# Two more places for expert panels: 23 in place of 21, from the scratch for dynamic DMAs

## The chip, the cores and the metric

The kernel runs on one core of one Trainium2 chip. The metric is the time of one execution on the device in microseconds, taken as the median of several runs. The core has TensorE for matrix products, VectorE, ScalarE and GpSimd for the rest, SyncE (SP), which here issues nearly all loads, and 16 DMA engines. Its on-chip memory, SBUF, has 128 partitions.

## What is computed

Two layers over 256 tokens of width 1024, in float32, batch 1. The first layer is a hybrid of a sparse latent attention (16 heads, top 64 keys) and a gated linear recurrence; the second has two attentions (MLA and MoBA, 8 heads each) and a mixture of 32 experts, of which each token uses two. Cut to what matters:

```python
def reference(x, ...):
    x = first_block(x, ...)     # x + (g_a * y_attn + g_r * y_rnn) @ w_out, then rms_norm
    return second_block(x, ...)

def second_block(x, ...):
    ...
    x = x + mixed @ w_out[l]
    x = x + hierarchical_moe(rmsnorm(x, ffn_norm[l]), ..., w_exp_gate[l], w_exp_up[l], w_exp_down[l])
    return rmsnorm(x, final_norm)

def expert_block(args):         # once for each expert, with its own three weights
    xb, e = args
    return (jax.nn.silu(xb @ w_g[e]) * (xb @ w_u[e])) @ w_d[e]
```

Each expert has a gate and an up weight of 1024 x 256 and a down weight of 256 x 1024. The weights of all 32 experts are read, 96 MB (3 MB for each expert), and the weights of the dense stages are another 70 MB.

## The kernel before

The dense weights come in 70 panels of 1 MB (`w_dense[p]`, 128 x 2048), each of two units of 128 x 1024. They go through the first four slots of `ring` (`DRING = 4`). ScalarE copies a unit into a rounded form (line 1165), GpSimd takes the difference between unit and rounded form (line 1579), and TensorE multiplies three times with these parts (`mm3`, line 509). Each unit that TensorE finishes raises `unit_done`. Dense panel p is loaded when the units of the panel in its slot are done: `dense_laps(a, b)` (line 404) does so in a loop, four slots a lap.

The expert weights come in 96 panels of 1 MB (`w_expert[q]`, `PANELS = 96`), six for each pair of experts: four with the gate and up weights (two halves of the depth for each expert), two with the down weights. They go through `wide_ring` (line 244), a list of `NSLOT` = 21 places of 8 KB per partition. Panel q uses place q mod `NSLOT`. The list holds tensors that the dense stages need earlier and that have become free: `wu`, parts of `small` and `big`, `scr`, `hT`, `attn`, the constants, the slots of `ring`, and `xT`. `expert(q)` (line 411) loads a panel, `expert_half(q, k)` (line 414) half of one, and `expert_panel(eng, q)` (line 360) is the wait of its reader. `in_halves` names the panels of the first filling that are loaded in two halves.

SP issues everything in one written order: the loads of the start (lines 389 to 400), then laps of dense panels with an expert panel between them where a place becomes free. `expert(0)` stands behind the keys of the first layer, `expert(1)` and `expert(2)` in the second layer, the other 18 towards the end of the dense stages. From line 470 on come the reloads, q from 21 to 95 in steps of two: each waits until `panel_used` says that panels q-21 and q-20 have been used. TensorE raises `panel_used` in `gate_up_half` (line 982), `sw_transposes` (line 972), `down` (line 1033) and `add_experts` (line 1073). Behind the last panel comes the last gain (line 488), 512 KB, which VectorE reads in the output stage (`layer_out`, line 2088).

In the expert layer TensorE goes through 16 pairs. A pair has two halves of gate and up products (line 993), two transposes, the down products (line 1041) and the sum into the output's banks (`add_experts`, line 1076); the next group's tokens are gathered between (line 968). The last two pairs also have idle products (`idle_products`, line 999), whose results nobody reads. The last pair's down products are those of `last_down` (line 1047).

Semaphores of the small weights: `s_in["wuk"]` and `s_in["wuv"]` for two loads into `wu`, `s_in["wkr"]` and `s_in["wrt"]` for two more.

The kernel is built with the default scratch for dynamic DMAs, 16 KB per partition of SBUF, which lies ahead of all tensors.

Of the kernel before, what the change touches and what calls it, by code (L numbers as in the profile page):

```python
# [30 lines left out]
P = 128  # L31
T = 256
NT = T // P
D = 1024
DC = D // P
# [24 lines left out]
PANELS = 3 * NE  # L60
CAUSAL = P + T

UNIT = 1024
RING = 6
DRING = 4
# [14 lines left out]
FILL0, UNIT0, UNITS_AT, RELEASE = {}, {}, [], []  # L80
# [40 lines left out]
def build(nc, x_t, vecs, consts, w_rg, w_uk, w_uv, w_kr, w_router, w_dense, w_expert, final_row, out):  # L121
    ctx = ExitStack()
    with ctx:
        def sb(name, shape, dt=F32):
            return ctx.enter_context(nc.sbuf_tensor(name, shape, dt))

        def sem(name):
            return ctx.enter_context(nc.semaphore(name))
# [3 lines left out]
        def sb2(name, shape):  # L132

            offset = -(-nc.sbuf_base // 32) * 32
            t = sb(name, shape)
            rounded[name] = nc.alloc_sbuf_tensor_at(f"{name}_r", shape, F32R, offset=offset)
            return t
# [18 lines left out]
        stat = sb("stat", [P, 2, 3, 2])  # L156
        th = sb("th", [P, 2, 2 * T])
        small = sb2("small", [P, 5 * 1024])

        def at(region, off, *dims):  # L160
            n = 1
# [74 lines left out]
        def xe_block(g, half, couple):  # L236
# [4 lines left out]
        x1_sq = at(small, 2 * K, DC, T)  # L241
        ye = at(small, 3 * K, 2, 512)
        sel = wkr.rearrange("p c n -> p (c n)").rearrange("p (a b c) -> p a b c", a=2, b=NT)
        wide_ring = [wu[:], small[:, 0:2 * K], big[:, 16 * K + 512:18 * K + 512], scr.rearrange("p c t -> p (c t)"), hT.rearrange("p c t -> p (c t)"),
                     attn[:, 0:2 * UNIT], cst[:, CST["center"]:CST["center"] + 2 * K],
                     big[:, 4 * K:6 * K], big[:, 6 * K:8 * K], big[:, 0:2 * K],
                     big[:, 14 * K:16 * K], big[:, 12 * K:14 * K], ring[:, 2, :], ring[:, 3, :], ring[:, 0, :],
                     ring[:, 4, :], ring[:, 1, :], ring[:, 5, :], big[:, 10 * K:12 * K], big[:, 2 * K:4 * K],
                     xT.rearrange("p c t -> p (c t)")]
        NSLOT = len(wide_ring)  # L250
        last_gain = wide_ring[12][:, 0:D]
        in_halves = {14, 15, 16, 17, 20}
        last_couple = 6 * (PAIRS - 1)
        rt = at(small, 4 * K, 1024)

# [3 lines left out]
        def C(name, n, i=0):  # L259
# [6 lines left out]
                                          for n in ("D0", "D1", "L0", "L1", "TB", "QB", "OB", "UB")]  # L266
# [13 lines left out]
        SPLITS = ("x0", "x", "u", "o", "m1", "x1", "att2", "wkr", "cq", "ck", "ob", "oa", "m2")  # L280
        hi_of = {n: sem(f"{n}_rounded") for n in SPLITS}
        lo_of = {n: sem(f"{n}_rest_ready") for n in SPLITS}
        s_in = {n: sem(f"in_{n}") for n in ("x0", "x1", "vec", "cst", "wrg", "wuk", "wuv", "wkr", "wrt",
                                            "first_unit", "last_gain")}
        unit_done, panel_used = sem("unit_done"), sem("expert_panel_used")
        rel = {"act": sem("bank_released_by_act"), "dve": sem("bank_released_by_dve")}
# [97 lines left out]
        @block.sync  # L384
        def _(sp_):
            def panel(slot, src):
                return sp_.dma_start(ring[:, slot, :], src).then_inc(arrived[slot], 16)

            sp_.dma_start(vec[:], vecs).then_inc(s_in["vec"], 16)
            sp_.dma_start(dense_unit(0), w_dense[0][:, 0:UNIT]).then_inc(s_in["first_unit"], 16)  # L390
            sp_.dma_start(xT[:, 4:8, :], x_half(1)).then_inc(s_in["x1"], 16)
            sp_.dma_start(dense_unit(1), w_dense[0][:, UNIT:2 * UNIT]).then_inc(arrived[0], 16)
            sp_.dma_start(cst[:, 0:NCST], consts).then_inc(s_in["cst"], 16)
            for p in range(1, DRING):
                panel(p, w_dense[p])
            sp_.dma_start(wrg, w_rg.rearrange("p (a c t) -> p a c t", a=2, c=8)).then_inc(s_in["wrg"], 16)
            sp_.dma_start(wuk, w_uk.rearrange("p (c t) -> p c t", c=8)).then_inc(s_in["wuk"], 16)
            sp_.dma_start(wuv, w_uv.rearrange("p (c t) -> p c t", c=16)).then_inc(s_in["wuv"], 16)
            sp_.dma_start(wkr[:], w_kr.rearrange("p (c t) -> p c t", c=DC)).then_inc(s_in["wkr"], 16)
            sp_.dma_start(wrt[:], w_router.rearrange("p (c t) -> p c t", c=DC)).then_inc(s_in["wrt"], 16)  # L400

            laps = DENSE_PANELS // DRING - 1

            def dense_laps(a, b):
                with sp_.Fori(a, b) as lap:
                    for slot in range(DRING):
                        sp_.wait_ge(unit_done, lap * (2 * DRING) + (2 * slot + 2 - 2 * DRING))
                        sp_.dma_start(ring[:, slot, :], w_dense[bass.ds(lap * DRING + slot, 1)].rearrange(
                            "a p n -> p (a n)")).then_inc(arrived[slot], 16)

            def expert(q):
                sp_.dma_start(wide_ring[q % NSLOT], w_expert[q]).then_inc(earrived[q % NSLOT], 16)

            def expert_half(q, k, arrival=None):
                part = np.s_[:, k * UNIT:(k + 1) * UNIT]
                sp_.dma_start(wide_ring[q % NSLOT][part], w_expert[q][part]).then_inc(arrival or earrived[q % NSLOT], 16)

            lap_keys = UNIT0["aproj"] // (2 * DRING) + 1
            lap_latents = UNIT0["qb"] // (2 * DRING) + 2
            lap_rotated = UNIT0["gates"] // (2 * DRING) + 1  # L420
            dense_laps(1, lap_keys)
            sp_.wait_ge(kk_mm, H1 // 2)
            expert(0)
            dense_laps(lap_keys, lap_latents)
            sp_.wait_ge(unit_done, UNIT0["qb"])
            expert(1)
            dense_laps(lap_latents, lap_rotated)
            sp_.wait_ge(maxed, H1 + 1)
            expert(2)
            dense_laps(lap_rotated, laps)  # L430

            def dense(p):
                sp_.wait_ge(unit_done, 2 * (p - DRING) + 2)
                panel(p % DRING, w_dense[p])

            left = list(range(laps * DRING, DENSE_PANELS))
            dense(left.pop(0))
            dense(left.pop(0))
            sp_.wait_ge(unit_done, UNIT0["omoba"])
            expert(3)  # L440
            expert(4)
            dense(left.pop(0))
            dense(left.pop(0))
            sp_.wait_ge(o_mm, H1 + 2 * H2)
            expert(5)
            expert(6)
            expert(7)
            dense(left.pop(0))
            expert(8)
            dense(left.pop(0))  # L450

            sp_.wait_ge(unit_done, UNIT0["out2"])
            expert(9)
            expert(10)
            sp_.wait_ge(mixed, 8)
            expert(11)
            for q, units in ((12, 134), (13, 136)):
                sp_.wait_ge(unit_done, units)
                expert(q)
            for q in (14, 16):  # L460
                for k in range(2):
                    sp_.wait_ge(unit_done, 137 + q - 14 + k)
                    expert_half(q, k)
                    expert_half(q + 1, k)
            expert(18)
            expert(19)
            for k in range(2):
                sp_.wait_ge(x2_in, 2 * k + 2)
                expert_half(20, k)
            for q in range(NSLOT, PANELS, 2):  # L470
                freed = 2 * (q - NSLOT)
                if q in in_halves:
                    for k in range(2):
                        sp_.wait_ge(panel_used, freed + 2 * k + 2)
                        expert_half(q, k)
                        expert_half(q + 1, k)
                else:
                    sp_.wait_ge(panel_used, freed + 4)
                    for n in range(q, min(q + 2, PANELS)):
                        if n in second_half:  # L480
                            expert_half(n, 0)
                            if n != last_couple + 2:
                                if n == last_couple + 3:
                                    expert_half(n - 1, 1, second_half[n - 1])
                                expert_half(n, 1, second_half[n])
                        else:
                            expert(n)
            sp_.wait_ge(panel_used, 2 * (PANELS - 2 * NSLOT + 22))
            sp_.dma_start(last_gain, final_row).then_inc(s_in["last_gain"], 16)

            for tt in range(NT):
                sp_.wait_ge(out_scaled, tt + 1)
                sp_.dma_start(out[:, (2 * tt + 1) * 512:(2 * tt + 2) * 512], y_out[:, tt, 512:1024]).then_inc(stored, 16)
            sp_.wait_ge(stored, 16 * 2 * NT)
# [3 lines left out]
        def _(pe):  # L498
# [178 lines left out]
                   wu[:, UNIT + (n % 2) * 512:UNIT + (n % 2 + 1) * 512], start=True, stop=True).then_inc(v1_mm, 1)  # L677

            pe.wait_ge(s_in["wrg"], 16)
            pe.wait_ge(s_in["wuv"], 16)  # L680
            for c in range(8):
                chunk("q", c, h2, between=(lambda i: rg_gates(3 * c - 16 + i)) if c >= 6 else None)
                if 2 <= c < 6:
# [51 lines left out]
                else:  # L735
                    chunk("rproj", rtodo.pop(0), (u_hi, u))

            pe.wait_ge(s_in["wuk"], 16)
            kept(pe, "q", 3)
            pe.wait_ge(v1_ready, 4)  # L740
            pe.wait_ge(widx_ready, 1)
# [166 lines left out]
            for i in range(4):  # L908
                half_chunk("omla", i, (oa_hi, oA))
            pe.wait_ge(padz, 1)  # L910
            pe.wait_ge(s_in["wrt"], 16)

            def route(i):

# [670 lines left out]
        def _(dve):  # L1585
# [284 lines left out]
            fold(cq_sq, 1, SQ0[N_CQ] + 2)  # L1870
            dve.wait_ge(sq, SQ0[N_CQ] + 3)
            v.tensor_tensor(cq_sq[:, 0:2, :], cq_sq[:, 0:2, :], cq_sq[:, 4:6, :], ALU.add).then_inc(cq_folded, 1)
            dve.wait_ge(s_in["wkr"], 16)
            split("wkr", wkr, wkr_hi, 0, DC)
            dve.wait_ge(s_in["wrt"], 16)
            v.tensor_tensor(wrt[:], wrt[:], V("ffn_norm_2", 0, 8).unsqueeze(2).to_broadcast([P, DC, NG + NE]),
                            ALU.mult).then_inc(padz, 1)

# [384 lines left out]
```

## Time and profile before

| | |
|---|---|
| median of 3 runs | 707.6 us (707.43 to 707.69) |
| span of the profiled execution | 705.3 us |
| TensorE (PE) busy | 660.1 us, 94% |
| GpSimd (POOL), VectorE (DVE), ScalarE (ACT) busy | 379.2, 335.9, 326.9 us |
| data moved by DMA | 181.71 MB, mean 258 GB/s |
| chain that ended last | PE 80%, DMA 14% |

The profile is of one execution; the page gives its span, and no time around it, so the median is set beside the span. Lines with SPq are instructions of SP's queue, which issues loads; the second number is how long the issue took, not the transfer. PEclk is TensorE's granted clock, 1.00 for 2.4 GHz and 0.50 for 1.2 GHz. The DMA share is the mean busy share of the 16 DMA engines in a window; rounding can take it to 1.01 and above. A number in square brackets at the end of a line is idle time ahead of the instruction and what ended it.

### The profile page before, as it was taken

The numbers are of one execution on the slowest core, as the hardware profiler recorded it, in microseconds if no ns is written. First come the engines' busy times: TensorE is split into PE (matmuls) and PEld (weight loads), VectorE is DVE, ScalarE is ACT, GpSimd is POOL, SyncE is SP. The second block draws the span as 40 slices with busy tenths as digits, with TensorE's granted clock in tenths as the row PEclk, the third lists the DMA queues.
The fourth block names the chain that finished last, engine by engine and source line by source line (L and its number), as shares of the span: only waits on it lengthen the run. The fifth ranks groups of instructions, "written<-read, shape, count | busy, mean of one in ns | idle before, by whom it ended". The sixth has DMA issues, their size and how long they took to land.

```text
span 705.3 us, 13837 instructions
## 1 busy us (share of the span) xinstructions
PE 660.1 (94%) x5608; PEld 550.3 (78%) x5608; DVE 335.9 (48%) x684; ACT 326.9 (46%) x603; POOL 379.2 (54%) x284
## 2 busy tenths in 40 slices
PE   5999999999999999999999999999999998687894
PEld 4899899999999999998899999999654544343442
DVE  5869723787871247895754554443422121121102
ACT  6566777866554456664358655442311111010104
POOL 3988557798887989998697555882000000000000
PEclk9999999999999999999999999999999999999998
DMA  8845334435346555464457334799899999999994
GB/s 341 322 168 180 119 121 132 168 122 172 125 158 210 184 189 188 158 245 166 141 167 285 126 120 157 309 425 388 346 423 419 422 422 419 423 423 420 422 419 162
DMA packets 27281, 181.71 MB, mean 258 GB/s; under 512 B 3024, under 2 KB 3280, under 8 KB 6864
## 3 DMA queue, kind: packets, MB, share of 16 engines
q1 hardware_dynamic: 26784, 179.74, 66.4%
q8 instruction: 47, 0.77, 0.5%
q10 hardware_dynamic: 432, 1.05, 0.4%
q14 instruction: 18, 0.15, 0.1%
HBM read 179.73 MB, written 1.05 MB: 256 GB/s over the span
## 4 chain that ended last, share of the span: by engine, by line
PE 80%; DMA 14%; ACT 2%; DVE 2%; issue 0%; POOL 0%; SPq 0%; ACTq 0%; DVEq 0%
PE D L512 49%; PE L L993 5%; DMA cst<-w_expert_dram 4%; DMA big<-w_expert_dram 4%; DMA ring<-w_expert_dram 4%; PE L L968 3%; PE L L696 2%; PE QB L1041 2%; PE D L560 2%; DMA ring<-w_dense_dram 2%; PE TB L705 2%; PE D L1076 1%; PE L L1002 1%; PE TB L1076 1%; PE L L668 1%; PE D L564 1%
## 5 line engine op out<-in xcount | busy, mean ns | idle before, releaser
L1579 POOL TENSOR_TENSOR ring_r<-ring,ring_r 128x512 fp32r<-128x512 f32 (+1 forms) x280 | 379.0, 1388 | 100.2 <-ACT ring_r L1165 99.7
L512 PE MATMUL D<-scr_r,ring_r 128*128 128x256 f32 x1104 | 214.0, 289 | 0.0
L1165 ACT ACTIVATE ring_r<-ring 128x1024 fp32r<-128x1024 f32 (+2 forms) x140 | 145.1, 1042 | 93.4 <-PE D L512 80.4
L512 PEld LDWEIGHTS D<-scr_r,ring_r 128*128 128x128 f32 x1104 | 175.6, 191 | 2.4 <-issue 1.6
L512 PE MATMUL D<-hT_r,ring_r 128*128 128x256 f32 x552 | 156.1, 283 | 0.0
L512 PE MATMUL D<-big_r,ring_r 128*128 128x256 f32 x1086 | 134.1, 284 | 1.7 <-POOL ring_r L1579 1.7
L512 PEld LDWEIGHTS D<-big_r,ring_r 128*128 128x128 f32 x1086 | 131.3, 192 | 3.4 <-POOL ring_r L1579 2.4
L512 PEld LDWEIGHTS D<-hT_r,ring_r 128*128 128x128 f32 x552 | 105.7, 192 | 1.1 <-issue 0.7
L1596 DVE SCALAR_TENSOR_TENSOR th<-th,L 64x256 f32<-64x256 f32 x32 | 13.4, 418 | 128.2 <-ACT th L1501 127.7
L1501 ACT ACTIVATE th<-L 64x256 f32<-64x256 f32 x16 | 6.0, 377 | 84.5 <-PE L L993 84.5
L993 PE MATMUL L<-big,small 128*32 128x256 f32 x384 | 34.5, 395 | 5.5 <-DMA ring<-w_expert_dram 3.0
L968 PEld LDWEIGHTS L<-wkr,big 128*128 128x128 f32 x240 | 27.9, 191 | 10.6 <-issue 9.9
L1321 ACT ACTIVATE attn<-TB 128x384 f32<-128x384 f32 x32 | 15.7, 491 | 39.0 <-PE TB L705 39.0
L968 PE MATMUL L<-wkr,big 128*128 128x128 f32 x240 | 30.6, 281 | 0.6 <-DVE wkr L2016 0.6
L1596 DVE SCALAR_TENSOR_TENSOR big<-big,D 128x512 f32<-128x512 f32 x16 | 11.0, 685 | 38.0 <-PE D L512 38.0
L1504 ACT ACTIVATE root<-OB 128x128 f32<-128x128 f32 x16 | 4.4, 278 | 52.7 <-PE OB L1030 52.7
L993 PEld LDWEIGHTS L<-big,small 128*32 128x32 f32 x384 | 17.3, 113 | 14.3 <-issue 7.7
L1313 ACT ACTIVATE L<-L,stat 128x128 f32<-128x128 f32 x64 | 25.1, 393 | 3.3 <-DVE stat L1726 3.2
L993 PE MATMUL L<-ring,small 128*32 128x256 f32 x256 | 21.2, 403 | 5.7 <-DMA ring<-w_expert_dram 2.9
L2053 DVE TENSOR_TENSOR small<-L,vec 128x256 f32<-128x256 f32 x30 | 11.3, 419 | 27.9 <-PE L L968 27.9
L1735 DVE TENSOR_SCALAR attn<-L,stat 128x128 f32<-128x128 f32 x64 | 23.8, 413 | 1.1
L1507 ACT ACTIVATE small<-QB 128x512 f32<-128x512 f32 x15 | 9.0, 597 | 30.6 <-PE QB L1041 30.6
(393 smaller groups left out, 1014.7 us busy)
## 6 DMA issues: line engine op xcount, KB each, us to landing
ring<-w_dense_dram SPq DMA_DIRECT2D x69, 1024.0 KB, 5.0
big<-w_expert_dram SPq DMA_DIRECT2D x35, 1024.0 KB, 23.8
ring<-w_expert_dram SPq DMA_DIRECT2D x20, 1024.0 KB, 26.2
wu<-w_expert_dram SPq DMA_DIRECT2D x5, 1024.0 KB, 24.4
small<-w_expert_dram SPq DMA_DIRECT2D x5, 1024.0 KB, 21.7
scr<-w_expert_dram SPq DMA_DIRECT2D x5, 1024.0 KB, 24.7
hT<-w_expert_dram SPq DMA_DIRECT2D x5, 1024.0 KB, 26.4
attn<-w_expert_dram SPq DMA_DIRECT2D x5, 1024.0 KB, 26.6
```

The source lines that it names most:

```text
L512: last = mm(out_, r32(w[i][ws]), r32(x[j][xs_]), start=start and m == 0, stop=stop and m == 2)
L560: mm(bank[:, u * T:(u + 1) * T], r32(w[h][:, k * P:(k + 1) * P]), r32(src[0][:, k, :]), start=(u + k + h == 0), stop=False, skip_group_che ...
L696: last = mm(LB[j][:, c0:c0 + n], q_of(j, tt), k_of(j, n), start=True, stop=True)
L705: last = nc.tensor.transpose(TB[:, b * P:(b + 1) * P], E[:, a % 2, b * P:(b + 1) * P], ident)
L968: last = mm(into[:, c * P:(c + 1) * P], htok[:, tt, (c0 + c) * P:(c0 + c + 1) * P], sel[:, g % 2, tt, :], start=(tt == 0), stop=(tt == NT ...
L993: last = mm(G[at_:at_ + WIN, 0:FF], x(4 * h + k, e), w[e][:, k, m, :], start=(h + k == 0), stop=(h * 4 + k == DC - 1))
L1165: A_(r32(hi_unit(j)[w]), dense_unit(j)[w], ACT.Copy).then_inc(hi_ready, 1)
L1313: last = A_(LB[a % 2][:, c0:c0 + n], LB[a % 2][:, c0:c0 + n], ACT.Exp, bias=stat[:, a % 2, 0, tt:tt + 1], accum_out=stat[:, a % 2, 1, tt:t ...
L1321: A_(PT[:, a % 2, :], TB[:, 0:CAUSAL], ACT.Copy).then_inc(pt_ready, 1)
L1579: last = g.tensor_tensor(r32(w), w, r32(h).bitcast(F32), ALU.subtract)
L1596: return v.scalar_tensor_tensor(out=out_, in0=in0, scalar=scalar, in1=in1, op0=op0, op1=op1)
L1735: last = v.tensor_scalar(E[:, a % 2, c0:c0 + n], LB[a % 2][:, c0:c0 + n], stat[:, a % 2, 2, tt:tt + 1], None, ALU.mult)
```

## The change

A tensor `spare` of two places is added, and the scratch for dynamic DMAs is set to 1024 bytes, which frees 15 KB of the 16 KB that it needs. The two places go to the front of `wide_ring`, so `NSLOT` is 23 and each old place has a number two higher. Panels 0 and 1 are loaded into them in the first layer, behind the first lap of dense panels (`UNIT0["gattn"]` is 22, so `lap_spare` is 2); each old place of the first filling gets the panel with a number two higher at the old point. The reloads run from 23 to 95. The last gain goes to the place of panel 73. Two pairs of small loads share a semaphore each, and their readers wait for both.

```diff
+        spare = sb("spare", [P, 2, 2 * UNIT])
...
-        wide_ring = [wu[:], small[:, 0:2 * K], big[:, 16 * K + 512:18 * K + 512], ...
+        wide_ring = [spare[:, 0, :], spare[:, 1, :], wu[:], small[:, 0:2 * K], big[:, 16 * K + 512:18 * K + 512], ...
...
-        last_gain = wide_ring[12][:, 0:D]
-        in_halves = {14, 15, 16, 17, 20}
+        last_gain = wide_ring[(PANELS - NSLOT) % NSLOT][:, 0:D]
+        in_halves = {16, 17, 18, 19, 22}
...
-            sp_.dma_start(wuk, w_uk.rearrange("p (c t) -> p c t", c=8)).then_inc(s_in["wuk"], 16)
-            sp_.dma_start(wuv, w_uv.rearrange("p (c t) -> p c t", c=16)).then_inc(s_in["wuv"], 16)
-            sp_.dma_start(wkr[:], w_kr.rearrange("p (c t) -> p c t", c=DC)).then_inc(s_in["wkr"], 16)
-            sp_.dma_start(wrt[:], w_router.rearrange("p (c t) -> p c t", c=DC)).then_inc(s_in["wrt"], 16)
+            sp_.dma_start(wuk, w_uk.rearrange("p (c t) -> p c t", c=8)).then_inc(s_in["wuk_wuv"], 16)
+            sp_.dma_start(wuv, w_uv.rearrange("p (c t) -> p c t", c=16)).then_inc(s_in["wuk_wuv"], 16)
+            sp_.dma_start(wkr[:], w_kr.rearrange("p (c t) -> p c t", c=DC)).then_inc(s_in["wkr_wrt"], 16)
+            sp_.dma_start(wrt[:], w_router.rearrange("p (c t) -> p c t", c=DC)).then_inc(s_in["wkr_wrt"], 16)
...
+            lap_spare = UNIT0["gattn"] // (2 * DRING)
...
-            dense_laps(1, lap_keys)
+            dense_laps(1, lap_spare)
+            expert(0)
+            expert(1)
+            dense_laps(lap_spare, lap_keys)
             sp_.wait_ge(kk_mm, H1 // 2)
-            expert(0)
+            expert(2)
...
-            sp_.wait_ge(panel_used, 2 * (PANELS - 2 * NSLOT + 22))
+            sp_.wait_ge(panel_used, 2 * (PANELS - NSLOT + 1))
             sp_.dma_start(last_gain, final_row).then_inc(s_in["last_gain"], 16)
...
-            pe.wait_ge(s_in["wuv"], 16)
+            pe.wait_ge(s_in["wuk_wuv"], 32)
...
-            dve.wait_ge(s_in["wkr"], 16)
+            dve.wait_ge(s_in["wkr_wrt"], 32)
...
-    nc = bacc.Bacc("TRN2", target_bir_lowering=False, num_devices=1)
+    nc = bacc.Bacc("TRN2", target_bir_lowering=False, num_devices=1, dynamic_dma_scratch_size=1024)
```

## Rows read from the trace of the kernel before

**Rows 1.** Windows of all engines by stage, the first line naming the columns.
```profile
core 0: us, PE busy (x) PEld busy (x) DVE busy (x) ACT busy (x) POOL busy (x), PEclk, DMA share, GB/s
500.00:580.00 80.00, 77.08 (x848) 42.10 (x840) 20.17 (x67) 11.69 (x31) 0.00 (x0) 1.00 0.98 405
580.00:660.00 80.00, 60.24 (x610) 31.02 (x614) 10.88 (x33) 8.51 (x22) 0.00 (x0) 0.94 1.01 422
660.00:692.00 32.00, 30.90 (x254) 13.80 (x250) 3.67 (x10) 5.20 (x12) 0.00 (x0) 0.98 1.00 411
```

**Rows 2.** Timeline of TensorE, 590 to 660 us: instructions behind a wait for a panel.
```profile
start us, us, engine line op out<-in xcount [idle before <-releaser]
597.48 1.93 PE L993 MATMUL L<-ring,small 128*32 128x256 f32 x32 [2.94 <-DMA ring<-w_expert_dram]
...
607.41 1.93 PE L993 MATMUL L<-big,small 128*32 128x256 f32 x32 [1.22 <-DMA big<-w_expert_dram]
...
613.44 0.61 PE L993 MATMUL L<-xT,small 128*32 128x256 f32 x1 [4.10 <-DMA wu<-w_expert_dram]
...
628.32 0.38 PE L993 MATMUL L<-attn,small 128*32 128x256 f32 x1 [2.68 <-DMA cst<-w_expert_dram]
...
643.20 0.38 PE L993 MATMUL L<-big,small 128*32 128x256 f32 x1 [3.04 <-DMA ring<-w_expert_dram]
...
658.15 0.61 PE L993 MATMUL L<-ring,small 128*32 128x256 f32 x1 [2.73 <-DMA big<-w_expert_dram]
```

**Rows 3.** Chain that ended last, in order of time: start, us, what.
```profile
658.15 3.40 PE L L993 x32
...
692.95 0.86 PE L L1056 x16
```

**Rows 4.** Timeline of SP's queue (issues of loads); below, a landing from the DMA view.
```profile
501.81 0.33 SPq L412 DMA_DIRECT2D wu<-w_expert_dram  x1
...
594.62 2.13 SPq L412 DMA_DIRECT2D hT<-w_expert_dram  x1
...
675.06 2.13 SPq L489 DMA_DIRECT2D ring<-final_row_dram  x1
...
ring<-final_row_dram SPq DMA_DIRECT2D x1, 512.0 KB, 19.1
```

**Rows 5.** Windows of all engines where the reloads begin.
```profile
500.00:502.00 2.00, 2.00 (x34) 1.10 (x27) 0.95 (x6) 0.00 (x0) 0.00 (x0) 1.00 0.14 51
502.00:504.00 2.00, 2.00 (x32) 1.45 (x34) 1.61 (x8) 0.00 (x0) 0.00 (x0) 1.00 0.53 131
```

**Rows 6.** The page: DMA queue with share; issues with median us to landing.
```profile
q1 hardware_dynamic: 26784, 179.74, 66.4%
...
ring<-w_expert_dram SPq DMA_DIRECT2D x20, 1024.0 KB, 26.2
```

**Rows 7.** SP's and ScalarE's timelines, landing of the loads of line 408, a window.
```profile
39.31 0.33 SPq L408 DMA_DIRECT2D ring<-w_dense_dram  x1
48.48 0.33 SPq L408 DMA_DIRECT2D ring<-w_dense_dram  x1
57.04 1.06 ACT L1165 ACTIVATE ring_r<-ring 128x1024 fp32r<-128x1024 f32 x1 [0.51 <-PE D L512]
DMA to landing us min/median/max: 4.7/4.8/4.9
40.00:50.00 10.00, 10.00 (x88) 9.16 (x87) 7.15 (x22) 8.10 (x16) 6.89 (x7) 1.00 0.38 116
```

**Rows 8.** A landing from the DMA view, and TensorE's timeline: first value product.
```profile
wrt<-w_router_dram SPq DMA_DIRECT2D x1, 144.0 KB, 18.8
...
68.30 1.02 PE L676 MATMUL OB<-wu,small 128*128 128x512 f32 x2
```

**Rows 9.** Windows of all engines behind two of the waits.
```profile
614.00:616.00 2.00, 2.00 (x25) 0.98 (x21) 0.00 (x0) 0.00 (x0) 0.00 (x0) 0.50 1.03 430
658.00:660.00 2.00, 1.85 (x20) 1.07 (x24) 0.00 (x0) 0.00 (x0) 0.00 (x0) 0.50 1.02 430
```

More of the change, by code:

```diff
@@ L243, in build @@
         sel = wkr.rearrange("p c n -> p (c n)").rearrange("p (a b c) -> p a b c", a=2, b=NT)
-        wide_ring = [wu[:], small[:, 0:2 * K], big[:, 16 * K + 512:18 * K + 512], scr.rearrange("p c t -> p (c t)"), hT.rearrange("p c t -> p (c t)"),
+        wide_ring = [spare[:, 0, :], spare[:, 1, :], wu[:], small[:, 0:2 * K], big[:, 16 * K + 512:18 * K + 512], scr.rearrange("p c t -> p (c t)"), hT.rearrange("p c t -> p (c t)"),
                      attn[:, 0:2 * UNIT], cst[:, CST["center"]:CST["center"] + 2 * K],
@@ L282, in build @@
         lo_of = {n: sem(f"{n}_rest_ready") for n in SPLITS}
-        s_in = {n: sem(f"in_{n}") for n in ("x0", "x1", "vec", "cst", "wrg", "wuk", "wuv", "wkr", "wrt",
+        s_in = {n: sem(f"in_{n}") for n in ("x0", "x1", "vec", "cst", "wrg", "wuk_wuv", "wkr_wrt",
                                             "first_unit", "last_gain")}
@@ L420, in _ @@
             lap_rotated = UNIT0["gates"] // (2 * DRING) + 1
-            dense_laps(1, lap_keys)
+            dense_laps(1, lap_spare)
+            expert(0)
+            expert(1)
+            dense_laps(lap_spare, lap_keys)
             sp_.wait_ge(kk_mm, H1 // 2)
-            expert(0)
+            expert(2)
             dense_laps(lap_keys, lap_latents)
             sp_.wait_ge(unit_done, UNIT0["qb"])
-            expert(1)
+            expert(3)
             dense_laps(lap_latents, lap_rotated)
             sp_.wait_ge(maxed, H1 + 1)
-            expert(2)
+            expert(4)
             dense_laps(lap_rotated, laps)
@@ L439, in _ @@
             sp_.wait_ge(unit_done, UNIT0["omoba"])
-            expert(3)
-            expert(4)
+            expert(5)
+            expert(6)
             dense(left.pop(0))
@@ L444, in _ @@
             sp_.wait_ge(o_mm, H1 + 2 * H2)
-            expert(5)
-            expert(6)
             expert(7)
+            expert(8)
+            expert(9)
             dense(left.pop(0))
-            expert(8)
+            expert(10)
             dense(left.pop(0))
             sp_.wait_ge(unit_done, UNIT0["out2"])
-            expert(9)
-            expert(10)
+            expert(11)
+            expert(12)
             sp_.wait_ge(mixed, 8)
-            expert(11)
-            for q, units in ((12, 134), (13, 136)):
+            expert(13)
+            for q, units in ((14, 134), (15, 136)):
                 sp_.wait_ge(unit_done, units)
                 expert(q)
-            for q in (14, 16):
+            for q in (16, 18):
                 for k in range(2):
-                    sp_.wait_ge(unit_done, 137 + q - 14 + k)
+                    sp_.wait_ge(unit_done, 137 + q - 16 + k)
                     expert_half(q, k)
                     expert_half(q + 1, k)
-            expert(18)
-            expert(19)
+            expert(20)
+            expert(21)
             for k in range(2):
                 sp_.wait_ge(x2_in, 2 * k + 2)
-                expert_half(20, k)
+                expert_half(22, k)
             for q in range(NSLOT, PANELS, 2):
@@ L736, in fill @@
                     chunk("rproj", rtodo.pop(0), (u_hi, u))
-            pe.wait_ge(s_in["wuk"], 16)
+            pe.wait_ge(s_in["wuk_wuv"], 32)
             kept(pe, "q", 3)
@@ L910, in _ @@
             pe.wait_ge(padz, 1)
-            pe.wait_ge(s_in["wrt"], 16)
+            pe.wait_ge(s_in["wkr_wrt"], 32)
             def route(i):
@@ L1872, in _ @@
             v.tensor_tensor(cq_sq[:, 0:2, :], cq_sq[:, 0:2, :], cq_sq[:, 4:6, :], ALU.add).then_inc(cq_folded, 1)
-            dve.wait_ge(s_in["wkr"], 16)
+            dve.wait_ge(s_in["wkr_wrt"], 32)
             split("wkr", wkr, wkr_hi, 0, DC)
-            dve.wait_ge(s_in["wrt"], 16)
+            dve.wait_ge(s_in["wkr_wrt"], 32)
             v.tensor_tensor(wrt[:], wrt[:], V("ffn_norm_2", 0, 8).unsqueeze(2).to_broadcast([P, DC, NG + NE]),
```

## The prediction

> **What bounds the kernel now.** I read the stages first, then TensorE's waits inside the last stage, then the queue that feeds it.
>
> The windows by stage [rows 1] split the last 200 us in three. From 500 to 580 TensorE is busy 77.08 of 80 us and the DMA engines 98% of the time: both run nearly full. From 580 to 660 the DMA engines have a share of 1.01 and move 422 GB/s, and TensorE is busy only 60.24 of 80 us: here the stream of expert panels sets the pace. From 660 to 692 both are full again. This is the expert layer: 96 panels of 1 MB pass through 21 places, and TensorE eats six of them (one pair of experts) in less time than the DMA engines bring six.
>
> TensorE's own timeline [rows 2] has seven waits for a panel between 597 and 658 us, of 2.94, 1.22, 4.10, 2.68, 1.20, 3.04 and 2.73 us (the fifth, at 638.23, isn't shown), 17.91 us in all, and none after 658.15. Four of them end at 613.44, 628.32, 643.20 and 658.15: 14.88, 14.88 and 14.95 us apart. Between two of them lies the work of one pair of experts, so six panels arrive in 14.9 us, 2.48 us each. The bandwidth says the same: 1,048,576 bytes at 422 GB/s are 2.485 us, and I take that.
>
> The chain that ended last [rows 3] tells what follows. From 658.15 TensorE works without a wait for data to the last down products at 692.95; then come the sums, squares, scale and store, to the span's end at 705.3. The chain doesn't show that the last panel is due at the same moment. The last gain, issued behind it at 675.06, lands after 19.1 us, at 694.2 [rows 4]. It is half a megabyte, 1.24 us at this rate, so the second half of panel 95 lands at about 692.9, and TensorE wants it in the second half of the products that begin at 692.95. So the last stage has two ends that meet within half a microsecond, TensorE's work behind 658.15 and the last byte of the stream, and both hang on the stream.
>
> **The change part by part.**
>
> *Two panels fewer in the stream.* Before, panels 0 to 20 are loaded ahead and 75 go into places that must be freed first; after, 23 and 73. What counts is when these reloads start and how fast they run. They start when TensorE has used panels 0 and 1: the first is issued at 501.81 [rows 4], and that doesn't depend on how many places there are. The loads ahead stay where they are, with numbers two higher: place k of before is place k+2 of after and is filled at the same point of the program. In the windows [rows 5] the DMA engines have nothing left at 500 (share 0.14), take up the reloads until 504 (0.53), and are full from there on. SP runs ahead of them: the issue at 501.81 took 0.33 us, that at 594.62 took 2.13 us, as long as the queue needs to make room [rows 4], and loads into the ring land 26.2 us after their issue [rows 6], some ten panels later. So the stream is limited by its rate, not by free places, and panel q arrives when q-2 arrived before: 2 x 2.485 = 4.97 us earlier. The bounds are 4.96 us (a third of 14.88) and 5.10 us (at the 411 GB/s of the last window of [rows 1]).
>
> Does TensorE follow? I replay its timeline [rows 2] with arrivals 4.97 us earlier. First wait: ready at 597.48 - 2.94 = 594.54, panels at 592.5, no wait. Second: ready at 607.41 - 1.22 - 2.94 = 603.25, panels at 602.4, none. Third: ready at 613.44 - 4.10 - 1.22 - 2.94 = 605.18, panels at 613.44 - 4.97 = 608.47: it waits 3.29 us, and from here on every time is that of before less 4.97. The last wait ends at 653.18, the last panel lands at 687.9, and the work behind them is unchanged. Gain: 4.97 us; 17.91 - 4.97 = 12.9 us of waits stay. What is late next is the same stream at the same place.
>
> *The two loads in the first layer.* They are issued behind the load of 39.31, the fourth of the first lap, so within a microsecond of it; the next load in the ring is issued at 48.48, when ten units are done, and SP has nothing to do between [rows 7]. A load alone lands after 4.8 us [rows 7]: the load of 39.31 at 44.1, and the two new ones, each 2.485 us later, at 46.6 and 49.1. The data of the load of 48.48 starts 4.8 - 2.5 = 2.3 us after its issue, when they are through. The window from 40 to 50 has a DMA share of 0.38 [rows 7], so 6.2 us free where 4.97 are wanted. If they did collide, the panel of 48.48 (landing at 53.3) is first read by ScalarE at 57.04 [rows 7]: 3.7 us of slack, and the rounding itself runs ahead of TensorE. Cost 0, the bound above is 4.97 - 3.7 = 1.3 us.
>
> *The scratch of 1 KB.* It moves every tensor 15 KB down and gives the room for the two places. All weights travel on queue q1, of kind hardware dynamic: 179.74 of 181.71 MB [rows 6]; no line of the kernel issues a DMA from GpSimd. Cost 0 by these rows, with a rival below. The Trainium skill, "DMA: Bandwidth & Descriptors", section "SWDGE vs HWDGE vs iDMA", says that this carveout holds the descriptor rings that GpSimd writes, and that loads from SP and ScalarE don't use it; by that page its size costs nothing, and no run here shows that yet.
>
> *The merged semaphores.* Each wait now ends with the later of two loads, all issued before 9 us; the last of the four lands 18.8 us after its issue, so by 28 us, and the first reader of any of them that I find is the value product at 68.30 [rows 8]. Cost 0.
>
> *The last gain* goes to the fifth place of the new list and waits for panel 73 rather than 75, but SP reaches that wait only behind the issue of panel 95, which waits for as much. It stays behind the stream and comes 4.97 us earlier. Cost 0. One loop on SP becomes two, in an idle stretch of 8 us. Cost 0.
>
> *Sum.* The profiled span 705.3 - 4.97 = 700.3 us. The median of the runs shown, 707.6, lies 2.3 us above the span; with the same 2.3 around it, 702.6 us. The Trainium skill, "DMA: Bandwidth & Descriptors", section "Bandwidth", puts the HBM side at about 358 GB/s per core when both cores of a domain stream; by that figure two panels would be worth an estimated 5.9 us and the time would be 701.7. The trace moves 422 GB/s with one core at work, and the sum goes by that.
>
> **The rivals.**
>
> *The clock falls once more behind the last wait.* TensorE's granted clock is 0.50, the lower of its two levels, in 614 to 616 and in 658 to 660, both right behind a wait for a panel [rows 9]. The 32 matmuls behind the wait of 607.41 took 1.93 us [rows 2], those behind 658.15 took 3.40 [rows 3]: 1.47 us lost. After the change the waits lie differently (two are gone, one is 3.29 in place of 4.10), so a drop can come at another moment. One is in the path already; one more between the last wait and the end costs 1.5 us, two cost 2.9: 704.1 to 705.5 us. Against it: from 660 to 692 TensorE is busy 30.90 of 32 us at a clock of 0.98 [rows 1]. If the present drop goes away, TensorE is 1.5 us earlier but the last panel isn't, and the gain grows by 0.3 at most, to 702.3. The Trainium skill, "TensorE: Matmul & The Clock Gate", section "HAM oscillation — how this bites in real kernels", says that waits for DMA between short bursts of products bring the slow clock back every time; the trace agrees in part, since after the wait of 607.41 the products ran at full speed.
>
> *The extra loads only push the others.* If they held up the dense ring and it never caught up, the 4.97 us would be spent there: 707.6 us. For it: the first layer is TensorE's and its ring is only four panels deep. Against it: 0.38 of the DMA engines used where the loads go.
>
> *Only part arrives*, because the reloads start later or with gaps: with half of the gain, 705.1 us. For it: the start of the reloads is set by a release, not by the rate [rows 4, 5]. Against it: nothing moves that release.
>
> *Slower: the small scratch limits the loads in flight.* If the 1 KB also held the descriptors of these loads, the ten or so in flight would become few. A load alone takes 4.8 us [rows 7] against 2.485 in the stream, so down to two in flight nothing is lost and below two it decides: with one, 73 x 4.8 = 350 us in place of 75 x 2.485 = 186, 164 us more, about 872 us. Against it: the kind of the queue [rows 6].
>
> *The change doesn't do what it says*: the two places are new memory, so nothing can be in the way of the early loads; if they were issued late instead, that is the case of the part gain.
>
> **How the numbers follow.** Forecast 702.6 (its own range 702.0 to 703.3): 0.77. A further drop of the clock (704.1 to 705.5): 0.10. Part of the gain (705.1): 0.05. No gain (707.6): 0.04. Slower, by the scratch or something that no row shows: 0.04. The range is 702.0 to 704.6: below, the bound of 5.10, the 0.3 of a missing drop and the spread of 0.26 us of the runs; above, one further drop. A measurement of this kernel can tell about 0.2%, 1.4 us, from no change. Faster by more: 0.91; within: 0.05; slower by more: 0.04.
>
> **What would show it.** In the profile after: the first reload issued at 501.8 as before; DMA share 1.01 and 422 GB/s until about 685 in place of 690; TensorE's first wait for a panel near 608, five waits in all of about 13 us, the last ending near 653.2; two expert loads issued behind 39.3 and the ring's next still at 48.5. The prediction is wrong if the stage until 500 is longer, if the products behind 653 run at the low clock for longer than before, or if loads of the expert stream land after 5 us where 26 were usual.

## The result

The changed kernel takes 701.98 us (median of 4 runs, 701.08 to 702.66) beside 707.51 us for the kernel before (706.80 to 707.69): ratio 0.9922, with a 95% interval of 0.9900 to 0.9944. That is 5.5 us less, between 4.0 and 7.1. The direction and the mechanism were forecast; the size, 4.9 to 5.0 us, was too small by half a microsecond, and the median lies 0.02 us below my range. The profiled execution took 701.36 us with a span of 699.6 us, so some 1.8 us lie around the span, not 2.3 as I had set from a span and a median of different executions. My sum takes the 2.3 off and adds it again, so this changes nothing in it.

The windows of the profile after, with the columns of [rows 1]; the second and third stage are taken 5 us earlier than there:

```profile
500.00:580.00 80.00, 77.07 (x840) 41.73 (x832) 19.40 (x61) 11.68 (x31) 0.00 (x0) 1.00 1.00 411
575.00:655.00 80.00, 62.78 (x646) 33.55 (x642) 12.75 (x39) 8.78 (x23) 0.00 (x0) 0.96 1.01 422
655.00:687.00 32.00, 30.90 (x258) 13.88 (x254) 3.67 (x10) 5.19 (x12) 0.00 (x0) 0.99 0.98 401
```

The stream still moves 422 GB/s, and TensorE still waits for it: 62.78 of 80 us busy, against 60.24 before. TensorE's timeline, as in [rows 2], has six waits now, of 3.95, 2.64, 1.20, 3.02, 1.17 and 3.04 us, 15.0 us in all:

```profile
607.55 3.29 PE L998 MATMUL L<-ring,small 128*32 128x256 f32 x32 [3.95 <-DMA ring<-w_expert_dram]
622.41 0.38 PE L998 MATMUL L<-xT,small 128*32 128x256 f32 x1 [2.64 <-DMA spare<-w_expert_dram]
...
652.13 3.48 PE L998 MATMUL L<-big,small 128*32 128x256 f32 x32 [3.04 <-DMA big<-w_expert_dram]
```

The first two waits of before are gone. The last ends at 652.13 in place of 658.15: 6.02 us earlier, where I had said 4.97. SP's queue, as in [rows 4] and [rows 7], says where the rest comes from:

```profile
39.70 0.80 SPq L413 DMA_DIRECT2D spare<-w_expert_dram  x2
48.46 166.43 SPq L409 DMA_DIRECT2D ring<-w_dense_dram  x24
...
500.51 0.80 SPq L413 DMA_DIRECT2D spare<-w_expert_dram  x2
503.69 0.33 SPq L413 DMA_DIRECT2D wu<-w_expert_dram  x1
```

The two early loads go out at 39.7, and the next dense one still at 48.46. But the first reload goes out at 500.51, not 501.81. It waits for TensorE, and TensorE was earlier because of its clock. Windows of all engines in the routing stage ahead of the expert layer, first of the kernel before, then of after:

```profile
490.00:492.00 2.00, 2.00 (x13) 2.00 (x13) 1.08 (x9) 0.26 (x1) 0.00 (x0) 0.62 0.92 301
492.00:494.00 2.00, 2.00 (x12) 2.00 (x12) 1.76 (x12) 0.82 (x2) 0.00 (x0) 0.52 1.03 399
```

```profile
490.00:492.00 2.00, 2.00 (x20) 2.00 (x20) 1.12 (x9) 0.79 (x2) 0.00 (x0) 1.00 0.99 348
492.00:494.00 2.00, 2.00 (x19) 1.86 (x17) 1.76 (x12) 1.53 (x3) 0.00 (x0) 1.00 1.01 397
```

The third number from the right is the granted clock: 0.62 and 0.52 before, 1.00 and 1.00 after. The first number in brackets counts TensorE's products: 25 in four microseconds before, 39 after. What I had to find out was whether the change did that, or chance.

Some single executions are delayed by 2 to 6 us (twelve of 64 of the kernel before, none of 16 of the changed kernel, one to three in each of five of its variants); the medians include them, and the profiles compared here are free of such a delay unless I say so.

### The profile page after: what moved, and what is told of

Same layout as the page of the kernel before. It is cut to its first block, busy times and chain, and to the rows that moved or that the text cites. A ratio compares the mean times of both kernels' runs of the same rounds, so it can differ in the third digit from the quotient of the medians.

```text
span 699.6 us, 13827 instructions
## 1 busy us (share of the span) xinstructions
PE 657.5 (94%) x5608; PEld 549.2 (79%) x5608; DVE 334.3 (48%) x684; ACT 326.8 (47%) x603; POOL 379.1 (54%) x284
## 4 chain that ended last, share of the span: by engine, by line
PE 83%; DMA 10%; DVE 2%; ACT 2%; issue 1%; SPq 0%; POOL 0%; ACTq 0%; DVEq 0%
PE D L517 49%; PE L L998 6%; DMA spare<-w_expert_dram 4%; DMA big<-w_expert_dram 4%; PE L L973 3%; PE QB L1046 3%; PE L L701 2%; PE D L565 2%; PE D L1081 2%; DMA ring<-w_dense_dram 2%; PE TB L710 2%; PE TB L1081 1%; PE L L1007 1%; PE L L673 1%; PE D L569 1%; PE D L548 1%
## 5 line engine op out<-in xcount | busy, mean ns | idle before, releaser
L998 PE MATMUL L<-big,small 128*32 128x256 f32 x368 | 31.9, 400 | 4.2 <-DMA big<-w_expert_dram 4.2
L998 PE MATMUL L<-ring,small 128*32 128x256 f32 x256 | 18.3, 406 | 4.0 <-DMA ring<-w_expert_dram 4.0
```

The lines of the kernel that those rows point to most:

```text
L998: last = mm(G[at_:at_ + WIN, 0:FF], x(4 * h + k, e), w[e][:, k, m, :], start=(h + k == 0), stop=(h * 4 + k == DC - 1))
```

## The experiments

The theories. *Stream*: the time is the bytes that the reload stream has to move, behind the moment at which it starts; two panels less are 4.97 us. *Chance*: the rest is TensorE's clock, which falls ahead of the reloads in some executions of either kernel. Against them: the change prevents the fall; the moved addresses or the small scratch bring a part; the number of places counts for something other than bytes; TensorE's work behind the last wait is the bound, not the stream.

**The changed kernel again, twice.** No edit.

> The changed kernel once more, with many runs beside the kernel before. Two theories for the 0.7 us beyond the 4.97 us of two panels. Clock by chance: TensorE's clock falls to 0.50 between 490 and 494 us in some executions and not in others, whichever kernel it is, and each fall costs 1.3 us; then single runs of either kernel lie in two groups 1.3 us apart (changed: about 701.2 and 702.6, before: about 706.3 and 707.6), each group with its own mean clock, and groups of the same clock differ by 5.0 us. The change removes the fall: the kernel before is always near 707.5 and the changed one always near 701.2, a gain of 6.3 us in fast pairs.

> The changed kernel once more, to stand beside the two below and to give more single runs for the two levels. If the fall of the clock before 494 us comes by chance in either kernel: again some runs near 701.3 and some near 702.6, and of before some near 706.2 and some near 707.4, like groups 4.8 to 5.0 us apart; the share of each group may be any.

Ratios 0.9923 (0.9908 to 0.9938) and 0.9923 (0.9907 to 0.9939), medians 702.09 and 702.14. With the four runs of the result there are 16 single runs of the changed kernel: seven from 700.99 to 701.85 (median 701.36), nine from 702.11 to 703.29 (702.60). Of 64 runs of the kernel before, 21 lie from 705.38 to 706.80 (median 706.18), 31 from 706.95 to 708.27 (707.46), twelve from 709.22 to 712.54. So both kernels have a lower and an upper group 1.2 to 1.3 us apart. They aren't sharply divided, and I drew the lines at 706.85 and at 702.1 by eye. Like compared with like, the gain is 706.18 - 701.36 = 4.8 and 707.46 - 702.60 = 4.9 us. Without a line between the groups it is the same: the means, the twelve slowest left out, are 707.02 and 702.07, 4.95 us apart. That speaks for chance and against a fall that the change prevents. The printed clock of a run is only a loose sign of its group.

The profile of the first of the two has the fall, in the same place as before, and its last wait is 1.40 us later than in the profile after. Its windows, SP's queue and TensorE's timeline:

```profile
490.00:492.00 2.00, 2.00 (x17) 2.00 (x17) 1.01 (x8) 0.68 (x2) 0.00 (x0) 0.84 1.00 291
492.00:494.00 2.00, 2.00 (x11) 2.00 (x11) 1.76 (x14) 0.96 (x2) 0.00 (x0) 0.50 1.03 399
```

```profile
501.89 0.80 SPq L413 DMA_DIRECT2D spare<-w_expert_dram  x2
```

```profile
653.53 1.93 PE L998 MATMUL L<-big,small 128*32 128x256 f32 x32 [2.89 <-DMA big<-w_expert_dram]
```

Against the kernel before with the same fall (first reload at 501.81, last wait ending at 658.15) that is 4.62 us, with nearly the same start of the reloads. One of the two groups isn't always this fall, though. The second profile (702.57 us) has no fall at 490 and still a first reload at 502.11; it runs 1.1 to 1.6 us late from its first layer on, because of these windows:

```profile
18.00:20.00 2.00, 0.37 (x3) 0.37 (x4) 1.65 (x1) 1.87 (x3) 2.00 (x3) 1.00 0.98 414
20.00:22.00 2.00, 2.00 (x13) 2.00 (x12) 1.93 (x6) 0.45 (x1) 2.00 (x2) 0.53 1.02 430
22.00:24.00 2.00, 2.00 (x13) 2.00 (x12) 2.00 (x7) 0.00 (x0) 2.00 (x3) 0.62 1.00 406
```

The clock fell at 20 us, behind a wait of 1.98 us for a rounded unit. In the profile after that wait was 1.40 us, in the first repeat 1.67, and the clock stayed at 1.00. So a fall of the clock in another place delays the reloads as well, and a run may have one of the two falls or none; no profile here has both.

**The scratch alone.**

```diff
-    nc = bacc.Bacc("TRN2", target_bir_lowering=False, num_devices=1)
+    nc = bacc.Bacc("TRN2", target_bir_lowering=False, num_devices=1, dynamic_dma_scratch_size=1024)
```

> The kernel before with its 21 places, only the scratch for dynamic DMAs set to 1 KB, so that all tensors lie 15 KB lower. If the gain is the stream's alone: 707.5 us, within 0.2 us of before, apart from the clock's fall. If the moved addresses or the smaller scratch bring part of it: 0.7 us less. If the scratch cost something that the two places outweigh: more than 708.

707.31 us beside 707.28, ratio 0.9986 (0.9967 to 1.0006). Its profile has the fall, the first reload at 501.82 and the last wait ending at 658.42, 0.27 us behind the kernel before. Neither the scratch's size nor the 15 KB by which the tensors move shows. The Trainium skill, "DMA: Bandwidth & Descriptors", section "SWDGE vs HWDGE vs iDMA", says that loads issued by SP and ScalarE don't use this scratch; this run agrees. The 0.27 us is what such profiles differ by in the same case, and with this one as the partner the gain of two places is 658.42 - 653.53 = 4.89 us.

**One place fewer, and one place more.** In the first, one spare place and one early load; in the second, the kernel before without `wu` in its list.

```diff
-        wide_ring = [spare[:, 0, :], spare[:, 1, :], wu[:], ...
+        wide_ring = [spare[:, 0, :], wu[:], ...
```

```diff
-        wide_ring = [wu[:], small[:, 0:2 * K], ...
+        wide_ring = [small[:, 0:2 * K], ...
```

> 22 places in place of 23: only one spare place, one expert panel loaded in the first layer, 74 panels in the reloads. Stream theory: half of the gain, 2.49 us less than before and as much more than with two, so about 705.0 (or 704.0 where the clock doesn't fall before 494 us). If the number of places counts for something else (a wait for a release that two places remove), the two halves differ.

> The kernel before with one place fewer: 20 places, 76 panels in the reloads. Stream theory: 2.49 us slower than before, like groups compared (708.7 and 709.9), so that 20, 21, 22 and 23 places lie on one line of 2.5 us each. If a release of a place held the stream up before, the step from 21 to 20 would be larger than that from 22 to 23.

With 20, 21, 22 and 23 places the medians are 709.96, 707.3 to 707.5, 704.24 and 702.1 us: steps of 2.6, 3.1 and 2.1, with the groups mixed in each. The profiles are sharper, since I can pair those of the same clock. With the fall at 490, the last wait ends at 658.15 and 658.42 with 21 places, 655.92 with 22 and 653.53 with 23: steps of 2.2 or 2.5, and of 2.4 us. Without the fall it ends at 659.66 with 20 and 652.13 with 23, 7.53 us for three panels, 2.51 each. TensorE's timelines and SP's queues (20 places, then 22):

```profile
659.66 0.38 PE L992 MATMUL L<-small 128*32 128x256 f32 x1 [3.02 <-DMA big<-w_expert_dram]
500.49 0.33 SPq L412 DMA_DIRECT2D small<-w_expert_dram  x1
```

```profile
655.92 1.93 PE L997 MATMUL L<-ring,small 128*32 128x256 f32 x32 [2.69 <-DMA ring<-w_expert_dram]
501.79 0.33 SPq L413 DMA_DIRECT2D spare<-w_expert_dram  x1
```

A place is worth one panel at the stream's rate, 2.4 to 2.5 us, and these runs show nothing else. The first reloads also settle what moves their start. Without the fall at 490 us they go out at 500.49 with 20 places and at 500.51 with 23; with it at 501.81 with 21, 501.79 with 22 and 501.89 with 23. So the start goes with the clock and not with the number of places. The fall is there with and without the change, and it is missing with the change and with 20 places, which have no part of it; so the change doesn't prevent it.

**The first reload held.** It waits until panels 2 and 3 are used too.

```diff
-                    sp_.wait_ge(panel_used, freed + 4)
+                    sp_.wait_ge(panel_used, freed + (8 if q == NSLOT else 4))
```

> The changed kernel, with the first reload held until panels 2 and 3 are used too, so it goes out at 503.7 in place of 500.5 or 501.9; nothing else waits longer. If the start of the reloads sets all behind it one for one, as two profiles of one kernel showed (1.38 us earlier start, last wait 1.40 us earlier): 1.8 to 3.2 us... that is the delay of the issue, 3.2 us, so about 705.2. If the splitting in halves failed because the start doesn't count: no change, 702.1.

705.55 us, ratio 0.9966 (0.9944 to 0.9989): 3.4 us above the changed kernel's 702.1. Its profile has the fall, so its partner is the first repeat. The first reload goes out at 504.74 in place of 501.89, 2.85 us later, and the last wait ends at 656.37 in place of 653.53, 2.84 us later. (I had expected the issue at 503.7, from a profile without the fall.)

```profile
504.74 0.80 SPq L413 DMA_DIRECT2D spare<-w_expert_dram  x2
```

```profile
656.37 1.93 PE L998 MATMUL L<-big,small 128*32 128x256 f32 x32 [3.04 <-DMA big<-w_expert_dram]
```

The windows from 500 to 510 us, first of the first repeat, then with the reload held, say the same in bytes:

```profile
500.00:510.00 10.00, 9.63 (x117) 5.73 (x120) 5.14 (x21) 1.49 (x4) 0.00 (x0) 1.00 0.74 288
```

```profile
500.00:510.00 10.00, 9.63 (x118) 5.79 (x114) 4.86 (x19) 1.81 (x5) 0.00 (x0) 1.00 0.45 165
```

The stream moved 123 GB/s x 10 us = 1.23 MB less, which are 2.9 us at 422 GB/s. A later start is passed on one for one over 150 us. That is how 1.3 us of clock in the routing stage come out at the end.

**The first reloads in halves.** If the start counts, an earlier one should help: the first halves of panels 23 and 24 go out when the first halves of 0 and 1 are used.

```diff
-        in_halves = {16, 17, 18, 19, 22}
+        in_halves = {16, 17, 18, 19, 22, 23, 24}
```

> The changed kernel, with the first two reloads (panels 23 and 24) split in halves, so that their first halves go out when the first halves of panels 0 and 1 are used, about 0.95 us earlier. If the start of the reloads sets everything behind it one for one, as I now think: the DMA engines idle 0.9 us less between 500 and 504, and the end comes 0.9 us earlier, about 701.0 at the median. If the start doesn't count (my prediction took it as fixed and never priced it) or two more issues cost as much: no change, 702.

It made the kernel slower: 703.27 us, ratio 0.9953 (0.9937 to 0.9969), 1.2 us above the changed kernel. The start is earlier, 499.79 in place of 500.51 in the profile after (neither has the fall), but the last wait ends at 653.30 in place of 652.13. The windows from 500 to 510, first of the profile after, then with the halves, say why:

```profile
500.00:510.00 10.00, 9.63 (x122) 5.76 (x114) 4.11 (x15) 1.87 (x5) 0.00 (x0) 1.00 0.88 345
```

```profile
500.00:510.00 10.00, 9.63 (x118) 5.77 (x114) 4.11 (x15) 1.87 (x5) 0.00 (x0) 1.00 0.81 289
```

In these 10 us the stream moved 2.89 MB in place of 3.45. The missing 0.56 MB are 1.3 us at 422 GB/s, and the last wait ended 1.17 us later. The same count fits the first repeat, which starts at 501.89: 288 GB/s in this window, 0.57 MB less than in the profile after or 1.4 us, and a last wait 1.40 us later. So it isn't the moment of the first issue that counts but the bytes moved once the ahead-of-time loads are through. (From 510 to 520 us all these profiles move 422 to 428 GB/s, and from there to 600 all move 421.) Why four half loads into an empty queue fill it worse than two whole ones, these runs don't say.

**The early loads later, and earlier.** Panels 0 and 1 loaded behind the last dense panel, and ahead of the first lap.

```diff
-            dense_laps(1, lap_spare)
-            expert(0)
-            expert(1)
-            dense_laps(lap_spare, lap_keys)
+            dense_laps(1, lap_keys)
...
+            expert(0)
+            expert(1)
             sp_.wait_ge(unit_done, UNIT0["out2"])
```

```diff
-            dense_laps(1, lap_spare)
             expert(0)
             expert(1)
-            dense_laps(lap_spare, lap_keys)
+            dense_laps(1, lap_keys)
```

> 23 places, but panels 0 and 1 are loaded at about 462 us, behind the last dense panel, where the DMA engines are full until 500, and not at 40 us. Stream theory (the engines' busy time from 455 us to the end sets the time, and only idle time in it is free): the 4.97 us come back, less the idle time between 500 and 504 (1.3 to 2.7 us) which the shifted loads fill: 2.3 to 3.7 us slower than the changed kernel, 704.4 to 705.8. If two more places were what helps, wherever they are filled: 702.1, as the changed kernel.

> 23 places, panels 0 and 1 loaded at 8.5 us, ahead of the first lap, where the DMA engines are full until 30 us. The fifth dense panel lands 5 us later, at 35 us in place of 30. Its first unit is wanted by TensorE at 40.6 and takes 3.7 us of rounding on ScalarE and GpSimd, which leaves some 2 us: if that slack holds, 702 to 703; if the rounding has no slack (GpSimd takes 2.6 us a unit against 2.9 on TensorE), it passes on and the whole kernel is up to 5 us later, 707.

Late: 703.65 us, ratio 0.9957 (0.9931 to 0.9984), 1.5 us above the changed kernel; in profiles without the fall the last wait ends at 654.17 in place of 652.13, 2.04 us later. The size was less than I expected. Windows with the late loads, and the profile after's first window for comparison:

```profile
455.00:500.00 45.00, 43.85 (x381) 42.39 (x384) 19.77 (x56) 18.45 (x28) 22.50 (x16) 1.00 1.01 419
500.00:510.00 10.00, 9.63 (x118) 5.76 (x114) 4.11 (x15) 1.87 (x5) 0.00 (x0) 1.00 1.01 420
```

```profile
455.00:500.00 45.00, 43.85 (x380) 42.39 (x383) 19.72 (x56) 18.35 (x28) 22.37 (x16) 1.00 1.01 409
```

The same count works: (420 - 345) x 10 us is 0.75 MB more in the gap at 500, (419 - 409) x 45 us is 0.45 MB more before it; of the 2.10 MB that were added, 0.90 MB remain, 2.1 us at 422 GB/s. A share of 1.01 is not always a full rate: 409 and 419 GB/s have the same share. I had missed this second reserve.

At the start: 702.22 us, ratio 0.9915 (0.9885 to 0.9944), as the changed kernel, and a span of 700.0 beside 699.6. The two loads land 21.3 and 21.5 us after their issue, by 33 us, and the fifth dense panel comes later: ScalarE begins to round it at 35.17 in place of 30.19. TensorE has no idle time from 25 to 50 us in either profile, so the slack that I had put at 2 us held. The first reload goes out 0.3 us later than in the profile after, about as much as such profiles differ by. My cost of 0 for the loads at 39.7 us was right with room to spare.

**The idle products left out.** The products of `idle_products` in the last two pairs aren't made; nobody reads their results.

```diff
-                    idle_products(4)
+                    idle_products(0)
...
-                        idle_products(2)
+                        idle_products(0)
```

> The changed kernel without the idle products of the last two pairs, whose results nobody reads (8.8 us of TensorE's time behind the last wait). If the last byte of the stream is the end that counts, as I read it (panel 95 lands within half a microsecond of its use): TensorE waits for panels again in that stretch and the time is the same within 0.5 us, or up to 1.5 us slower where the clock falls in these waits. If TensorE's work is the end that counts: up to 8.8 us faster, about 693.

702.26 us, ratio 0.9941 (0.9916 to 0.9966), and a span of 699.4 beside 699.6: no gain, though the idle products kept TensorE busy for 9.2 us in the profile after. Behind 652.21 TensorE waits again, 1.24, 3.03, 1.38 and 0.22 us, and the chain that ended last now ends in the last panel:

```profile
667.02 19.93 DMA small<-w_expert_dram
686.96 0.04 issue
687.00 0.64 PE L L1061 x8
```

So the stream's last byte is the end, as I had read from the landing of the last gain in [rows 4], and TensorE's work behind the last wait isn't. The repeats of the changed kernel say so too: in both the 32 products behind the last wait took 1.93 us in place of 3.48, and still 47.2 and 47.3 us lie between that wait and the span's end, against 47.5. The products that are only idle cost nothing here, and leaving them out brings nothing.

**A product against the fall.** One idle product of 256 columns ahead of the last token sums.

```diff
             sum_tokens(0)
             route(3)
             pe.wait_ge(sq, SQ0[N_FFN] + 4)
+            mm(L0[:, 0:T], ident, C("iota", T), start=True, stop=True)
             sum_tokens(6, 7).then_inc(ssq, 1)
```

> The changed kernel with one idle product of 128 x 256 (0.43 us) ahead of the last token sums, where TensorE's narrow products (36 columns and one) precede the fall of its clock. If keeping the array busy there prevents the fall between 490 and 494 us: the two groups of runs become one, at 701.4 + 0.4 = 701.8. If the fall comes all the same: two groups as before, each 0.4 us later, median 702.5.

702.34 us over seven runs from 700.75 to 707.50, no single group: inconclusive as a time. Its profile, of an execution that ran 4.4 to 5 us late from its first layer on, shows the fall all the same. The product begins at 493.75 us, and the windows behind it are:

```profile
494.00:496.00 2.00, 2.00 (x14) 1.95 (x14) 0.29 (x2) 0.26 (x1) 0.00 (x0) 0.75 1.00 340
496.00:498.00 2.00, 2.00 (x11) 2.00 (x11) 1.76 (x13) 0.69 (x1) 0.00 (x0) 0.50 1.02 381
```

So in this execution a product of this size at this place didn't prevent it; whether it makes the fall rarer, one profile can't say.

## Why the prediction came out as it did

The step that failed is the one sentence in the part on the stream: the first reload "is issued at 501.81, and that doesn't depend on how many places there are", and the rival of a part gain's "nothing moves that release". The number of places doesn't move it, but the clock does, by 1.3 us, and I had looked for the clock's falls only behind the last wait. I never opened the windows at 490 us, where the trace of before had one on the path to the release. The first three runs shown lay within 0.26 us of each other, and I took that for the kernel's spread. All three, and the profile, were of the upper group; over 64 runs it is the lower and upper groups together, 2.9 us wide without the slowest, that one has to allow for. The changed kernel's four runs had two of each group, which moved their median down by half a step, 0.65 us. With the groups in the sum the range would have begun near 701. That these four runs fell just outside the range is luck of the draw: the median of all 16 is 702.14, inside it. The sum set out from three runs of the upper group of the kernel before, and its 702.6 is where the upper group of the changed kernel lies (702.60).

The other steps, by the runs:

- Two panels less are 4.97 us: held. 4.62 and 4.89 us by profiles of the same clock, 4.8 and 4.9 by groups of runs, and 2.4 to 2.5 us for each place from 20 to 23. The small shortfall isn't settled; profiles of the same case differ by 0.3 us. The measured 5.5 us (4.0 to 7.1) doesn't exclude 4.97.
- TensorE follows: held, with a last wait 4.97 us earlier plus the start's 1.30, less 0.25. There were six waits instead of five, and 15.0 us instead of 12.9: before, the clock fell behind the wait of 643.20, and TensorE then came to the next panels too late to wait; after, it didn't fall behind 637.28, and TensorE waited 1.17 us more at 647.16. Such a wait moves nothing.
- Two ends that meet: the stream's is the one that binds (no idle products, no gain).
- The loads in the first layer cost nothing: held, even at 8.7 us. The bound of 1.3 us wasn't needed.
- The scratch, the merged semaphores, the last gain: 0 within some 0.3 us; the scratch by its own run, the others only in the step from 21 to 22 places, which holds them and is 2.2 to 2.5 us like the rest.
- The rival of a further fall behind the last wait: the products there took 3.48 us in the profile after, one fall as before, and 1.93, no fall, in both repeats. It stayed out. A fall of the clock does move the time, but ahead of the reloads: right in kind, wrong in place.

A fall also comes behind the first wait for a panel in some profiles (3.29 us for 32 products at 607.55 in the profile after, 3.64 in the first repeat, against 1.93 in the second). There it costs nothing, since the next wait takes it up.

## What to carry to other kernels

Where a stream of loads sets the end, count bytes: everything moved before the stream's bound stretch begins comes off at the stream's rate (2.5 us for each MB here), wherever earlier the engines have room, and every idle microsecond at its start stays in the end. So look at what releases the first load of that stretch, and at TensorE's clock on the way there. And before a range of half a per cent is given, ask whether the few runs shown can be of one group only.

## What the runs showed of the hardware

The clock fell at 490 us in some executions and not in others of the same kernel with the same instructions: the group of products that begins at 490.23 us in the profile after begins at 490.35 in the first repeat, and from 490 to 494 there are 39 products in the one and 28 in the other, 1.4 us at the first reload. What decides it stays open.

The profiled execution of the last experiment took 707.50 us for a kernel of 702.3, and shows where such a delay can lie. Its VectorE timeline, and that of the profile after:

```profile
27.08 12.28 DVE L1621 TENSOR_TENSOR hT_r<-hT,scr_r 128x512 fp32r<-128x512 f32 x4
```

```profile
27.00 6.84 DVE L1620 TENSOR_TENSOR hT_r<-hT,scr_r 128x512 fp32r<-128x512 f32 x4
```

Four subtractions took 12.28 us in place of 6.84, with GpSimd busy beside them in both, and TensorE waited 2.27 us for them; the first of the early loads went out at 44.1 us in place of 39.7, and all later stages were as late. In the other twelve profiles these four took 5.80 to 6.89 us. The Trainium skill, "SBUF — State Buffer", section "Who interferes with whom", says that a VectorE instruction with two inputs in SBUF contends with GpSimd instructions that read it; that fits, and so does GpSimd's timeline, with seven instructions in 8.79 us from 25.76 on where the first repeat has six in 9.34. But one profile doesn't show that this is the cause, nor that the twelve runs above 709 us of the kernel before are of this kind.
